# A two-block transformer kernel: the second half of both down projections by token halves, the norms behind it split in two

## The reference

```python
x = x + gt2 * conv_glu_ffn(h, w_up, conv_w, conv_b, w_down)   # (silu(conv3(gate)) * val) @ w_down, D_FF = 2816
x = rms_norm(x, norm_final)                                   # x * rsqrt(mean(x*x) + 1e-6) * g, per token
```

```python
x = layer_norm(ALPHA * x + conv_ffn(x, w_up_2, ..., w_down_2), ln2_g, ln2_b)   # this is the output
```

## Time and profile before

| | |
|---|---|
| median of three runs | 2663.39 us |
| the profiled execution | 2664.73 us, its span 2662.9 us |
| TensorE busy (matmul) | 2486.4 us, 93% of the span |
| VectorE, ScalarE, GpSimd busy | 1452.2, 876.1, 871.6 us |
| mean granted TensorE clock | 0.96 |
| second down projection of block 0 | 1288.97 to 1407.8 us |
| second down projection of block 1 | 2497.27 to 2616.1 us |

### The profile page before, as it was taken

How to read it: one execution, slowest core, us unless ns; L and a number is a source line. 1 busy time by engine, 2 the same in 40 slices (tenths; PEclk the granted TensorE clock), 3 DMA queues, 4 the chain that set the end, 5 groups by cost and what they waited for, 6 DMA issues and landing times.

```text
span 2662.9 us, 36956 instructions
## 1 busy us (share of the span) xinstructions
PE 2486.4 (93%) x15164; PEld 1455.5 (55%) x15164; DVE 1452.2 (55%) x1697; ACT 876.1 (33%) x1082; POOL 871.6 (33%) x494
## 2 busy tenths in 40 slices
PE   5899999999889999999998889999888999999996
PEld 2555558886445555555554556675344555555552
DVE  5764666773486630566325687355486640466413
ACT  3255422221144520445213222321155531354303
POOL 0212110000236531555215767201226532455320
PEclk7999999999989999999998889989999999999998
DMA  7611020000301133111312612300111122211311
GB/s 322 236 41 44 17 107 3 3 3 16 118 9 64 48 105 125 64 48 59 118 69 104 103 48 70 136 1 24 56 72 48 64 87 104 87 64 48 118 33 63
DMA packets 53497, 196.29 MB, mean 74 GB/s; under 512 B 5585, under 2 KB 15313, under 8 KB 50385
## 3 DMA queue, kind: packets, MB, share of 16 engines
q1 hardware_dynamic: 45552, 176.38, 19.5%
q10 hardware_dynamic: 7776, 17.56, 1.9%
HBM read 164.55 MB, written 29.36 MB: 73 GB/s over the span
## 4 chain that ended last, share of the span: by engine, by line
PE 80%; DVE 10%; issue 2%; POOL 2%; DMA 2%; ACT 2%; SPq 0%; ACTq 0%; DVEq 0%; POOLq 0%
PE pt L1138 15%; PE pt L1144 15%; PE pt L1141 15%; PE pt L1680 11%; PE pt L573 7%; PE pt L411 3%; PE pt L714 2%; PE pt L2391 2%; PE pt L2397 2%; PE pt L2394 2%; DVE work L536 1%; PE pt L344 1%; DMA work<-in_w_mod 1%; PE pt L332 1%; PE pt L397 1%
## 5 line engine op out<-in xcount | busy, mean ns | idle before, releaser
L1088 POOL TENSOR_TENSOR slots<-work,weights_rounded 128x512 bf16<-128x512 f32 (+2 forms) x234 | 420.7, 1798 | 598.5 <-ACT weights_rounded L1247 309.0
L1141 PE MATMUL pt<-work,weights_rounded 128*128 128x512 bf16 x1248 | 334.8, 386 | 0.0
L1138 PE MATMUL pt<-rounded,weights_rounded 128*128 128x512 f32 x624 | 210.1, 453 | 15.8 <-POOL slots L1088 10.2
L1138 PE MATMUL pt<-rhs_rounded,weights_rounded 128*128 128x512 f32 x624 | 210.2, 453 | 12.0 <-POOL slots L1088 7.8
L573 PE MATMUL pt<-work 64*64 64x64 f32 (+5 forms) x4512 | 208.0, 240 | 6.5 <-DVE work L536 5.5
L1138 PE MATMUL pt<-hidden_rounded,weights_rounded 128*128 128x512 f32 x704 | 207.2, 427 | 0.4
L573 PEld LDWEIGHTS pt<-work 64*64 64x64 f32 (+3 forms) x4512 | 188.7, 138 | 26.0 <-DVE work L536 7.7
L1141 PEld LDWEIGHTS pt<-work,weights_rounded 128*128 128x128 bf16 x1248 | 100.1, 99 | 169.0 <-issue 98.1
L1144 PE MATMUL pt<-hidden_rounded,slots 128*128 128x512 bf16 x704 | 179.9, 387 | 0.0
L1141 PE MATMUL pt<-slots,weights_rounded 128*128 128x512 bf16 x704 | 174.4, 381 | 0.0
L1144 PE MATMUL pt<-rounded,slots 128*128 128x512 bf16 x624 | 171.2, 390 | 0.0
(11 more groups left out here) (368 smaller groups left out, 4112.2 us busy)
## 6 DMA issues: line engine op xcount, KB each, us to landing
work<-in_w_up SPq DMA_DIRECT2D x64, 512.0 KB, 4.0
work<-in_w_down SPq DMA_DIRECT2D x32, 704.0 KB, 4.0
work<-in_w_mod SPq DMA_DIRECT2D x10, 2048.0 KB, 8.7
slots<-in_w_in SPq DMA_DIRECT2D x31, 512.0 KB, 3.6
slots<-in_w_up SPq DMA_DIRECT2D x24, 512.0 KB, 4.8
x_scratch<-work ACTq DMA_DIRECT2D x16, 512.0 KB, 2.6
work<-x_scratch SPq DMA_DIRECT2D x16, 512.0 KB, 8.0
slots<-in_w_v SPq DMA_DIRECT2D x10, 512.0 KB, 4.3
```

The source lines that it names most:

```text
L1088: did(pool, pool.tensor_tensor(dst, raw, high.bitcast(F32), ALU.subtract), name)
L1138: pe.matmul(out, whi[:, k * P:k * P + P], rhs_hi(k), start=first and k == ks[0], stop=False, skip_group_check=True)
L1141: pe.matmul(out, top_half(whi)[:, k * P:k * P + P], rhs_lo(k), start=False, stop=False, skip_group_check=True)
```

## The change

In both blocks the down projection of half 1 runs as 16 half jobs i: first the eight output tiles of token half 0 (i = 0 to 7), then those of token half 1 (i = 8 to 15). Each half job has its own load, rounding and split of its weights, so that each row block of weights is loaded and split twice. Jobs 0 and 1 do ten k tiles each, then the eleventh of both; the rest does all eleven in one go. Each half job has one PSUM bank.

Between half jobs of token half 1 the norm of token half 0 is done, by the functions `norm_act`, `norm_dve` (block 0) and `end_act`, `end_dve` (block 1), called behind each half job, and on TensorE by `later[i]`. The norm of token half 1 comes behind job 15. In block 0, u0 and u1 get their token half 0 right behind job 15, and their token half 1 as before. In block 1 the output is stored by halves.

```diff
...
-            ffn_pe(pe, 0)
-            pe.wait_ge(E("ffn_added"), 16)
-            pe.wait_ge(E("square_sums"), 14)
-            token_sums(pe, "ssf", w(SQF[0]), const("ones")[:, 0:1], 1)
-            token_rows(pe, "rbf", ("rstd_sqrt", 3), one_row)
+            ffn_pe(pe, 0, {8: lambda: norm_sums(pe, 0), 9: lambda: norm_rows(pe, 0)})
...
-            rms_act(act, SQF, ("ffn_added", 8), 3)
+            ffn_act(act, 0, "ffn_conv_w", "ffn_conv_b", norm_act)
+
+        def norm_act(act, n):
+            h, m = divmod(n, 8)
+            act.wait_ge(E("ffn_added"), 8 + n + 1)
+            ins = act.activation(w(SQF[m])[:, half_of(h)], w(X + m)[:, half_of(h)], ACT.Square)
...
+            if n == 9:
+                half_wait(act, "dve", "yrecip")
+                half_did(act, act.activation(small(RS, 4), small(RS, 4), ACT.Sqrt), "act", "yroot")
+            for k in {10: (0, 1, 2), 11: (3, 4, 5), 12: (6, 7)}.get(n, ()):
...
+                half_did(act, act.activation(hi(H + k)[:, 0:512], w(X + k)[:, 0:512], ACT.Copy), "act", ("x2hi", k))
+            if n == 14:
+                act.wait_ge(E("ffn_w_used"), JOBS - 1)
+                split2_hi(act, 0)
+            if n == 15:
+                act.wait_ge(E("ffn_w_used"), JOBS)
+                split2_hi(act, 1)
+                act.wait_ge(E("rstd_recip"), 3)
+                did(act, act.activation(small(RS + 4, 4), small(RS + 4, 4), ACT.Sqrt), "rstd_sqrt")
+                for k in range(8):
...
+                    did(act, act.activation(hi(H + k)[:, 512:1024], w(X + k)[:, 512:1024], ACT.Copy), "rhs_hi")
...
+        def norm_dve(dve, n):
...
+            if m > 1:
+                total(m - 1)
+            if m == 7:
+                total(7)
+            if n == 8:
+                recip(0)
+            if n == 9:
+                normed(0)
+            if n == 15:
+                recip(1)
+                normed(1)
...
-        JOBS = HALF1 + 8
+        JOBS = HALF1 + 16
...
-                for m in range(8):
+                for m in range(16 if half else 8):
                     at = down_at(m)
                     pool.wait_ge(E("ffn_w_hi"), rounded_down(t, half, m) + 1)
                     low(flat_lo(at, WCOLS), down_raw(m), flat_hi(at, WCOLS), "ffn_w_split")
+                    if t == 0 and half == 1:
+                        for k in {12: (0, 1, 2), 13: (3, 4, 5), 14: (6, 7)}.get(m, ()):
...
+            def down_half(i, ks):
+
+                h, m = divmod(i, 8)
+                if ks[0] == 0:
+                    pe.wait_ge(E("ffn_w_split"), down_job(t, 1, i) + 1)
+                    if i < 8:
+                        pe.wait_ge(E("ffn_post"), 5 * fast_at(t, 1, FH - 2 + i // 4) + 5)
+                    else:
+                        pe.wait_ge(E("ffn_added"), 24 * t + 8 + i - 4 + 1)
...
+            for i in range(2):
+                down_half(i, range(FH - 1))
+            for i in range(2):
+                down_half(i, (FH - 1,))
+            for i in range(2, 16):
+                down_half(i, range(FH))
+                if i in later:
+                    later[i]()
...
+            for i in range(16):
+                if i < 14:
+                    high_down(1, i + 2)
+                later(act, i)
...
                 for n in range(2):
                     claim(pe, f"b2u{n}")
+                    pe.wait_ge(E("ffn_added"), 8 + 14 + 2 * n)
                     pe.wait_ge(E("w_split"), NJOBS1 + n + 1)
+                    for k in range(8):
+                        half_wait(pe, "pool", ("x2lo", k))
+                        mm(pt(f"b2u{n}")[:, first], weights(n, k)[0], hi(H + k)[:, first], k == 0, False)
...
+                    if n == 0:
+                        norm_sums(pe, 1)
+                    else:
+                        norm_rows(pe, 1)
...
+            ffn_pe(pe, 1, {8: lambda: mean(0), 10: lambda: squares(0), 11: lambda: columns(0), 12: lambda: rows(0)})
+            mean(1)
+            squares(1)
+            columns(1)
+            rows(1)
...
+            def end_act(act, n):
+                if n == 9:
+                    squares(0)
+                if n == 10:
+                    kept_row(0)
+                if n == 11:
+                    root(0)
+                if n in (12, 13):
+                    biased(0, range(4 * (n - 12), 4 * (n - 12) + 4))
+                if n == 15:
+                    squares(1)
+                    kept_row(1)
+                    root(1)
+                    biased(1, range(8))
...
+            def end_dve(dve, n):
+                h, m = divmod(n, 8)
+                if m > 0:
+                    total(h, m)
+                if n == 8:
+                    centered(0)
+                if n == 11:
+                    recip(0)
+                if n == 12:
+                    scaled(0)
+                if n == 15:
+                    centered(1)
+                    recip(1)
+                    scaled(1)
```

More of the change, by code:

```diff
@@ L1082, in ffn_sp @@
                 sp.dma_start(w(XB[t] + m), kept_x(t, m)).then_inc(E(f"x_load{m // 4}"), 16)
-            for m in range(4, 8):
+            for m in range(4, 16):
                 rows(1, m)
@@ new lines, in mixer2_pe, with mean @@
+            row_sums(pe, "lv1", range(26, 34), range(25, 33))
+            row_columns(pe, "lc1", "lv1")
+            token_rows(pe, "rl1", ("rstd_sqrt", 5), one_row)
+            def mean(h):
+                if h:
+                    pe.wait_ge(E("ffn_added"), 48)
+                    pe.wait_ge(E("x_sums"), 14)
+                else:
+                    half_wait(pe, "dve", ("xsum", 7))
+                pe.matmul(end_bank(1, 4 * h), const("ones"), w(XSUM[1])[:, half_of(h)], start=True, stop=True,
+                          skip_group_check=True).then_inc(E("pt_filled" if h else "half_pe"), 1)
@@ new lines, in squares @@
+            def squares(h):
+                for k in range(8):
+                    if h:
+                        pe.wait_ge(E("squares"), 32 + k + 1)
+                    else:
+                        half_wait(pe, "act", ("lsq", k))
+                    ins = pe.matmul(end_bank(1, 4 * h + 1)[0:1, :], const("ones")[:, 0:1], w(k)[:, half_of(h)], start=(k == 0),
+                                    stop=(k == 7), skip_group_check=True)
+                ins.then_inc(E("pt_filled" if h else "half_pe"), 1)
@@ new lines, in columns @@
+            def columns(h):
+                if h:
+                    pe.wait_ge(E("pt_emptied_act"), ordinal["lv2"])
+                else:
+                    half_wait(pe, "act", "row")
+                for st in range(4):
+                    at = 512 * h + st * P
+                    ins = pe.matmul(end_bank(1, 4 * h + 2)[:, st:st + 1], w(ROW)[0:1, at:at + P], const("ones")[0:1, 0:1],
+                                    start=True, stop=True, skip_group_check=True)
+                ins.then_inc(E("pt_filled" if h else "half_pe"), 1)
@@ new lines, in kept_row, with root @@
+            def kept_row(h):
+                filled(act, "lv2") if h else half_wait(act, "pe", "lv")
+                ins = act.activation(w(ROW)[0:1, half_of(h)], end_bank(1, 4 * h + 1)[0:1, :], ACT.Copy)
+                if h:
+                    did(act, ins, "pt_emptied_act")
+                else:
+                    half_did(act, ins, "act", "row")
+            def root(h):
+                rs = small(RS + 4 * h, 4)
+                if h:
+                    act.wait_ge(E("rstd_recip"), 6)
+                    did(act, act.activation(rs, rs, ACT.Sqrt), "rstd_sqrt")
+                else:
+                    half_wait(act, "dve", "lrecip")
+                    half_did(act, act.activation(rs, rs, ACT.Sqrt), "act", "lroot")
@@ new lines, in recip @@
+            def recip(h):
+                filled(dve, "lc2") if h else half_wait(dve, "pe", "lc")
+                rs = small(RS + 4 * h, 4)
+                ins = dve.tensor_scalar(rs, end_bank(1, 4 * h + 2)[:, 0:4], 1.0 / D, LN_EPS, ALU.mult, ALU.add)
+                V_(ins, "pt_emptied_dve" if h else "dve_step")
+                if h:
+                    V_(dve.reciprocal(rs, rs), "rstd_recip")
+                else:
+                    half_did(dve, dve.reciprocal(rs, rs), "dve", "lrecip")
```

378 lines of the change are left out of this document (254 added, 124 removed).

## The result

The changed kernel takes 2668.16 us (median of 20 runs), the kernel before in the same runs 2662.69: ratio 1.0022, 95% interval [1.0015, 1.0029], or +5.5 us where +6.7 was predicted. The profiled execution of after took 2667.08 us (span 2664.9), that of before 2664.73 (2662.9), so the two spans are 2.0 us apart where the medians are 5.5 apart.

What follows compares the result with a forecast made beforehand. The prediction took TensorE's stream to bound the kernel, full in both second down projections. First stage +15.2, first tail -5, second stage +17.5, last tail -21.0 gave +6.7 on 2663.4: 2670 us, 8-in-10 range 2656 to 2679.

Steps and rivals of the forecast that it cites:

- Part 1: Loop of 16 half jobs, both blocks: splits stay hidden; stalls and slow clock at the start cost 7.1 us per block.
- Part 2: First block's norm work inside TensorE's stream: sums 1.0, stall at job 9 4.0, rows 1.5, clock 1.6; 8.1 us.
- Part 3: First tail, up to the first S5 state matmuls: 5 us shorter, bounds 0 and -9.
- the collisions: First tail: VectorE's small operations slowed by GpSimd's x2 subtractions; of 6.6 us, 4 expected back.
- VectorE's chain starts about 1 us earlier: First tail: stores and next weight tile stay at the DMA limit, 12 us, so S5 coefficients start only about 1 us earlier.
- nothing comes back: Rival, first tail: x2 stores delay the third weight tile's load and subtractions still meet VectorE; +5, 2675 us; chance 0.20.
- the mixer starts with its tiles: Rival, first tail: TensorE's 14.5 us gain carries through to the S5 state matmuls; 2660 us; chance 0.17.
- Part 4: Second block: 17.5 us more in the stage, 21.0 us less in the last tail.
- The sum: Whole kernel: +15.2 - 5 + 17.5 - 21.0 = +6.7 us.
- The signs in the profile: Expected shifts: first block's last down matmul 15 us later, S5 gate about 10, second block's about 28, end 7.

Runs made afterwards that it cites:

- the other order: Changed kernel with ten tiles of job 0, five of job 1, job 0's eleventh, then job 1's rest: 2657.57 us, 0.9983 of the kernel before.
- the rows ahead of u1: Changed kernel with token half 1's four row matmuls directly behind its one-column sums, before tile u1's first half: 2662.38 us, 1.0003 of the kernel before.
- load 2 ahead: Changed kernel with SyncE's load of the mixer's third weight tile issued before the eight x2 stores: 2662.62 us, 1.0003 of the kernel before.
- the kernel before with load 2 ahead: Kernel before, with only the load of the mixer's third weight tile moved before the eight x2 stores: 2664.58 us, ratio 1.0009.

## Why the prediction was right

**Part 1, the loop and its start.** Right in each term: splits hidden in both blocks (the split at 1326.48 ends 2.25 us before its job begins; 2.4 was said), a gap of 0.87 where 1.2 was said, 4.14 where 4.3 was, 1.5 of clock where 1.6 was. The experiment with the other order shows that the long gap comes from the order of the first four pieces, not from the halving; the short one, for job 1's split, stays (0.86). Three drops of the clock, of 1.5, 1.9 and 1.5 us, make 4.9 of the 32 us by which the two stages grew. The Trainium skill ("TensorE: Matmul & The Clock Gate", section "HAM oscillation — how this bites in real kernels") says that an array which waits between bursts begins the next one at the slow clock. The rows agree behind 3.69 and 4.1 us, and show no drop behind 0.8 us (2.78 for eleven matmuls).

**Part 2, the stall at job 9.** 3.69 for 4.0. Its cause, ScalarE's place for the root, is shown by giving it one job more: the wait is gone. The sums added 1.0 to their job for 1.0, the rows 1.7 for 1.5 (start of the rows to start of the group behind: 1373.83 to 1375.56), the clock 1.9 for 1.6 in this profile, 0.9 and twice 0.5 in three others with the same stall. The 1.38 us drain beside a table load that the Trainium skill gives ("ScalarE: Activation LUTs", section "What ACT_TABLE_LOAD costs") isn't seen: with it the gap would be 5.4 by the prediction's sum, and in the rows of after the load at 1450.74 begins 0.01 us behind the rounding and the Exp 0.02 behind the load.

**Part 3, the first tail.** The mechanism held, its size was low: -8.0 for -5, within its bounds of 0 and -9. The start of VectorE's chain came to -2.6 for -1, the collisions to -5.1 for -4. The step that was too small is "VectorE's chain starts about 1 us earlier": I set it by the DMA engines' 12 us for 4.7 MB. The load of the third weight tile leaves SyncE's queue behind the eight stores, and these began 13.35 us behind the wake for 14.62 and were issued in 7.87 us instead of 9.54, since VectorE finishes half tiles in 6.2 us instead of 10.5. That is 2.9 us, and 2.6 arrived. The rival "nothing comes back" is dead: its condition was a load 2 later than 30 us behind the last matmul, and it came at about 27. The rival "the mixer starts with its tiles" is dead by the constant 42.4 us.

**Part 4, the second block.** The stage grew by 16.9 for 17.5. Its start cost 0.82 + 4.13 + 1.5 = 6.5 for 7.1. By the starts of the groups around them, the mean added 0.9 to the stream for 1.0, the squares 7.2 for 6.9, the columns 1.2 for 1.0 and the rows 0.8 for 1.5. Only the rows are off: I had halved a row of which most ran at the slow clock, and should have scaled it by the clock as I did the squares. Last tail -20.4 for -21.0.

**The sum.** It came out at +5.5 for +6.7, and that it is so near is in part luck. The pieces of the one profile give +3.1, 3.6 below the sum, mainly because the first tail gave 3 us more than I put. What brings the medians back up is how the two profiled executions lie to their medians, 3.1 us together, which no term of the prediction is about. The signs in the profile show the same shortfall: the first block's last down matmul comes 14.4 us later (15 said), but the gate only 6.3 (10), the second block's last down matmul 22.4 (28), and the end of the span 2.0 (7).

## What to carry to other kernels

Moving half of an epilogue into the stage ahead of it pays that half's matmuls in a full stream and takes them off the tail: a small gain at best (-3.4 us in the second block) until the stalls at its seams were gone, then about 10 us per block. So look at the first jobs (which slot comes free when) and at every place where another engine's queue order holds up the full one: a wait of 4 us cost 5.2 to 6.6 with the clock. And ask of each saving in a tail which chain starts the next stage: here it was a load behind eight stores and VectorE beside a busy GpSimd, not TensorE. An edit to that chain is worth what the engine beside it leaves: the same load moved ahead brought the gate 3.4 us forward with half tiles and 1.1 without.

## What the runs showed of the hardware

- **The same gap, two prices.** In the last tail TensorE idles 1.58 us ahead of the square sums in every kernel with the change. They took 8.65 to 8.72 us in the five with the old order of jobs 0 and 1, and 7.03 in the three with the new one. In that block the two kinds of kernel differ only in the order of jobs 0 and 1, more than 100 us earlier. Windows over the sums, of after and of the kernel with the other order, have the clock at 0.81 and 1.00:

```profile
2642.00:2651.00 9.00, 8.15 (x16) 1.41 (x16) 4.91 (x8) 5.04 (x8) 0.00 (x0) 0.81 0.00 0
```

```profile
2636.00:2643.00 7.00, 6.67 (x16) 1.25 (x16) 4.43 (x7) 4.69 (x8) 0.00 (x0) 1.00 0.00 0
```

  Likewise the group behind the 3.69 us gap took 4.79 us in after, 3.81 with the other order and 3.34 with the rows ahead of u1 or load 2 ahead. So a gap's clock price isn't a function of its length alone; what else sets it, these runs don't settle.
- **A collision slows only some of VectorE's operations.** Beside GpSimd's elementwise work some of VectorE's 0.19 us operations take 2.24 and others, between them, 0.18: 2.24, 0.18, 2.25 in the rows of the kernel before with load 2 ahead. Beside half tiles the held-up operations take 1.2. The held-up ones last nearly as long as one operation of GpSimd (2.46 and 1.36 us for one subtraction, 19.72 / 8 in before and 10.87 / 8 with load 2 ahead), which agrees with the Trainium skill, "SBUF — State Buffer", section "Terms", where the shared port is held for a whole instruction. Here smaller pieces on GpSimd made shorter waits on VectorE.
